# First attention's scores over all 128 rows, with key halves exchanged and queries doubled by on-chip transfers

## The reference, cut to what matters

```python
def project(t):                       # x: 256 tokens, context: 256 tokens
    p = t @ w_in                      # 1024 x 4096
    q, k, v, z = jnp.split(p, ...)    # q, k: 8 heads x 2 halves x 64; v: 8 heads x 128; z: 1024
q, k = apply_rope(q), apply_rope(k)   # x's tokens alone
k_all = concat([k, kc]); v_all = concat([v, vc])       # 512 keys

def diff(qq, kk, vv, gate):
    o1 = sweep_attention(qq[..., 0, :], kk[..., 0, :], vv)   # softmax(q k^T / 8) v
    o2 = sweep_attention(qq[..., 1, :], kk[..., 1, :], vv)
    o = rms_norm(o1 - lam * o2, subln_g) * (1 - lam_init)
    ...                               # times silu(z), then w_out
y = diff(q, k_all, v_all, z)          # x attends over x and context: 512 keys
yc = diff(qc, kc, vc, zc)             # context attends over context: 256 keys
```

## Time and profile before

| | |
|---|---|
| median of 3 runs | 780.48 us (780.07 to 780.59) |
| the profiled execution | 780.35 us, its span 778.3 us |
| TensorE busy (share of the span) | 765.4 us (98%), 4137 matmuls |
| TensorE weight loads | 613.8 us (79%) |
| VectorE | 550.9 us (71%) |
| ScalarE | 392.4 us (50%) |
| chain that ended last, by engine | TensorE 73%, VectorE 16%, ScalarE 3%, transfers 3% |
| of it, score matmuls of the first attention (L1067) | 3% |

### The profile page before, as it was taken

The page is one execution under the profiler, slowest core; times in us unless marked ns, Lnnn a source line. Parts: engine busy times, 40 slices in busy tenths (PEclk is TensorE's granted clock), DMA queues, the critical chain, the costliest instruction groups (busy, mean ns, idle before and its releaser), DMA issues.

```text
span 778.3 us, 11220 instructions
## 1 busy us (share of the span) xinstructions
PE 765.4 (98%) x4137; PEld 613.8 (79%) x4137; DVE 550.9 (71%) x985; ACT 392.4 (50%) x749; POOL 42.5 (5%) x55
## 2 busy tenths in 40 slices
PE   8999999999999999999999999999999999999998
PEld 6668777887777788867788888787788888888886
DVE  3456998987677867599757766998977554555553
ACT  4452222328788765566656656625444444444441
POOL 0120000000001010112100002200100000000000
PEclk9999999999999999999999999999999999999999
DMA  9995554333000085249222055963325855665621
GB/s 325 361 379 191 207 216 167 116 121 137 2 1 1 1 314 209 71 152 340 76 92 74 6 175 166 365 221 107 100 69 183 270 163 164 204 209 182 203 67 55
DMA packets 72409, 125.78 MB, mean 162 GB/s; under 512 B 2842, under 2 KB 36844, under 8 KB 71204
## 3 DMA queue, kind: packets, MB, share of 16 engines
q1 hardware_dynamic: 71504, 123.00, 45.9%
q10 hardware_dynamic: 388, 1.08, 0.4%
q0 software_dynamic: 464, 0.98, 0.4%
HBM read 123.99 MB, written 1.06 MB: 161 GB/s over the span
## 4 chain that ended last, share of the span: by engine, by line
PE 73%; DVE 16%; ACT 3%; DMA 3%; issue 2%; SPq 1%; POOL 1%; DVEq 0%; ACTq 0%
PE psum L871 15%; PE psum L873 14%; PE psum L872 14%; DVE w_lo L2004 5%; PE psum L1067 3%; PE psum L1092 3%; PE psum L1388 3%; PE psum L1387 3%; PE psum L1386 3%; PE psum L993 2%; PE psum L860 2%; PE psum L1165 2%; PE psum L861 2%; PE psum L862 2%; DMA kT<-in_ada_w 2%
## 5 line engine op out<-in xcount | busy, mean ns | idle before, releaser
L872 PE MATMUL psum<-w_lo,act_hi 128*128 128x512 f32 (+1 forms) x624 | 242.1, 388 | 0.0
L871 PE MATMUL psum<-w_hi,act_hi 128*128 128x512 f32 (+1 forms) x584 | 237.4, 407 | 2.9 <-DVE act_lo L2187 2.5
L873 PE MATMUL psum<-w_hi,act_lo 128*128 128x512 f32 (+1 forms) x584 | 226.9, 388 | 0.0
L2004 DVE TENSOR_TENSOR w_lo<-raw,w_hi 128x2048 fp32r<-128x2048 f32 (+1 forms) x68 | 153.2, 2261 | 62.3 <-ACT w_hi L1425 62.3
L1425 ACT ACTIVATE w_hi<-raw 128x2048 fp32r<-128x2048 f32 (+1 forms) x72 | 136.2, 1894 | 67.5 <-PE psum L873 30.9
L871 PEld LDWEIGHTS psum<-w_hi,act_hi 128*128 128x128 f32 x584 | 109.7, 188 | 37.7 <-issue 13.5
L872 PEld LDWEIGHTS psum<-w_lo,act_hi 128*128 128x128 f32 x624 | 117.5, 188 | 20.4 <-issue 0.5
L873 PEld LDWEIGHTS psum<-w_hi,act_lo 128*128 128x128 f32 x584 | 109.6, 188 | 23.3
L1973 POOL TENSOR_TENSOR rstd<-ms,half_neg 128x1 f32<-128x1 f32 (+3 forms) x38 | 36.0, 950 | 521.5 <-DVE ms L2045 521.5
L860 PE MATMUL psum<-act_hi,w_hi 128*128 128x512 f32 x128 | 50.7, 396 | 1.7 <-DVE w_lo L2004 1.7
L861 PE MATMUL psum<-act_lo,w_hi 128*128 128x512 f32 x128 | 50.0, 390 | 0.0
(11 more groups left out here) (295 smaller groups left out, 1123.0 us busy)
## 6 DMA issues: line engine op xcount, KB each, us to landing
raw<-in_a_w_in SPq DMA_DIRECT2D x16, 1024.0 KB, 8.7
raw<-in_ada_w SPq DMA_DIRECT2D x14, 1024.0 KB, 5.1
raw<-in_w_out SPq DMA_DIRECT2D x12, 1024.0 KB, 5.4
raw<-in_w_gate SPq DMA_DIRECT2D x22, 512.0 KB, 4.2
raw<-in_w_up SPq DMA_DIRECT2D x22, 512.0 KB, 5.3
raw<-in_w_down SPq DMA_DIRECT2D x11, 1024.0 KB, 4.9
raw<-in_b_w_in SPq DMA_DIRECT2D x10, 1024.0 KB, 7.5
raw<-in_w_in SPq DMA_DIRECT2D x10, 1024.0 KB, 6.0
```

The costliest lines, as they stand in the source:

```text
L871: pe.matmul(oh, x_hi, hi, start=(k == 0), stop=False)
L872: pe.matmul(o[:, 0:n], x_hi, lo, start=False, stop=False)
L873: mm = pe.matmul(oh, x_lo, hi, start=False, stop=(k == KT - 1))
L2004: ins = dve.tensor_tensor(rest, weights, hi.bitcast(F32), ALU.subtract)
```

## The change

Four pairs of heads have halves of their keys exchanged in place: what was the rounded part of the second half (rows 64 to 127 of `round_k`) and the rest of the first half (rows 0 to 63 of `rest_k`) change places, by way of `taken`. Then `round_k` of a head holds rounded and rest of its first half, one above the other on 128 rows, and `rest_k` those of its second half. The queries are laid out to match: for each pair of steps eight transfers write, for each half s, the rounded queries of that half on both the lower and the upper 64 rows, and the rests likewise, into one slot of `w_lo` that is kept for this by an entry `("doubled", 0, 0)` of the plan of loads. A step's scores are then, for each half, two matmuls on 128 rows: doubled rounded queries by (rounded, rest) keys, doubled rests by the same keys. This adds the product of rest by rest, which was left out before. All transfers are issued by SP, in its order between the weight loads; SP waits between the phases of an exchange. TensorE waits for the exchange of the heads and for the doubled queries before each step's scores.

```diff
@@ loads_plan
         if c == 4:
             plan += both("ada0g", 1)
+        elif c == 6:
+            plan.append(("doubled", 0, 0))
@@
+EXCHANGED_BEFORE = {("in0", 6, 0): [0, 1], ("doubled", 0, 0): [2], ("in0", 7, 0): [3]}
+
+
+DOUBLED_BEFORE = {("in0", 7, 1): [2], ("out0", 0, 0): [3], ("out0", 0, 1): range(4, 9), ("out0", 1, 0): range(9, 16)}
@@ emptied
-            if stage == "ada0g":
+            if stage == "doubled":
+                b, at = place[("s0", NT * HEADS - 1, 1)]
+                emptied[n] = (full[b], at + 1)
+            elif stage == "ada0g":
                 emptied[n] = (s_sumused, h + 1)
@@
+        LOW, HIGH = slice(0, 64), slice(64, P)
+        doubled_at = load_no[("doubled", 0, 0)] % RAW
+        doubled = w_lo[:, doubled_at, :].rearrange("p (s r i n) -> p s r i n", s=2, r=4, i=2)
@@ SP
+            def exchange(pair):
+                heads = slice(2 * pair, 2 * pair + 2)
+                last = HEADS + 2 * pair + 1
+                b, at = place[("in0", BY_FEATURES[0] + last // NT, last % NT)]
+                sp.wait_ge(s_rest0, last + 1)
+                sp.wait_ge(free[b], at + 1)
+                aside = taken[:].rearrange("p t n -> p (t n)").bitcast(F32)
+                for i, half in enumerate((LOW, HIGH)):
+                    sp.dma_start(aside[half], round_k[HIGH, 2 * pair + i, :].bitcast(F32)).then_inc(s_exchanged, 16)
+                sp.wait_ge(s_exchanged, 96 * pair + 32)
+                for h in (2 * pair, 2 * pair + 1):
+                    sp.dma_start(round_k[HIGH, h, :].bitcast(F32), rest_k[LOW, h, :].bitcast(F32)).then_inc(s_exchanged, 16)
+                sp.wait_ge(s_exchanged, 96 * pair + 64)
+                for i, half in enumerate((LOW, HIGH)):
+                    sp.dma_start(rest_k[LOW, 2 * pair + i, :].bitcast(F32), aside[half]).then_inc(s_exchanged, 16)
+                if pair < HALF_KT - 1:
+                    sp.wait_ge(s_exchanged, 96 * pair + 96)
+
+            def doubled_queries(pair):
+                t, h = STEPS0[2 * pair]
+                if pair == 0:
+                    sp.wait_ge(s_rest0, HEADS)
+                elif pair >= 2:
+                    b, at = place[("s0", 2 * pair - 3, 1)]
+                    sp.wait_ge(full[b], at + 1)
+                r = slice(2 * (pair % 2), 2 * (pair % 2) + 2)
+                tokens = round_q[:, h, :].rearrange("p (s t n) -> p s t n", s=2, t=XT)[:, :, t, :].bitcast(F32)
+                rests = rest_q[:, 2 * pair:2 * pair + 2, :].bitcast(F32)
+                for s, own in enumerate((LOW, HIGH)):
+                    for half in (LOW, HIGH):
+                        sp.dma_start(doubled[half, s, r, 0, :].bitcast(F32), tokens[own]).then_inc(s_doubled[pair % 2], 16)
+                        sp.dma_start(doubled[half, s, r, 1, :].bitcast(F32), rests[own]).then_inc(s_doubled[pair % 2], 16)
@@ SP, over the loads
+                for pair in EXCHANGED_BEFORE.get(loads[n], ()):
+                    exchange(pair)
+                if loads[n][0] == "doubled":
+                    sp.wait_ge(*emptied[n - RAW])
+                    for pair in range(2):
+                        doubled_queries(pair)
+                    continue
+                for pair in DOUBLED_BEFORE.get(loads[n], ()):
+                    doubled_queries(pair)
@@ TensorE, scores0
-                o = [begin(("s0", p, s)) for s in range(2)]
-                for i in range(3):
-                    for s in range(2):
-                        rows = slice(64 * s, 64 * s + 64)
-                        q = rest_q[rows, p, :] if i == 2 else round_q[rows, h, tile_cols(t)]
-                        k = (rest_k if i == 1 else round_k)[rows, h, keys]
-                        mm = pe.matmul(o[s][:, 0:n], q, k, start=(i == 0), stop=(i == 2))
-                        if i == 2:
-                            mm.then_inc(bank_full(("s0", p, s)), 1)
+                pe.wait_ge(s_doubled[p // 2 % 2], 128 * (p // 4 + 1))
+                pe.wait_ge(s_exchanged, 96 * (h // 2 + 1))
+                for s in range(2):
+                    o = begin(("s0", p, s))
+                    k = (round_k, rest_k)[s][:, h, keys]
+                    for i in range(2):
+                        mm = pe.matmul(o[:, 0:n], doubled[:, s, p % 4, i, :], k, start=(i == 0), stop=(i == 1))
+                    mm.then_inc(bank_full(("s0", p, s)), 1)
```

More of the change, by code:

```diff
@@ L302, in block_kernel @@
     load_no = {key: n for n, key in enumerate(loads)}
-    halves = [key for key in loads if not key[0].startswith("ada")]
+    halves = [key for key in loads if not key[0].startswith("ada") and key[0] != "doubled"]
     half_no = {key: g for g, key in enumerate(halves)}
@@ L450, in block_kernel @@
         s_gatein = sem("first_gate_chunk_in")
+        s_exchanged = sem("key_halves_exchanged")
+        s_doubled = [sem(f"doubled_queries{i}") for i in range(2)]
         N_CIN, N_VEC, N_LATE = 3, 4, 10
@@ L582, in block_kernel @@
         for n, (stage, c, h) in enumerate(loads):
-            n_landed[n % RAW] += 32 if stage == "gu" else 16
+            n_landed[n % RAW] += 32 if stage == "gu" else 0 if stage == "doubled" else 16
             landed_at[n] = n_landed[n % RAW]
```

## The result

The changed kernel takes 793.24 us (793.14 to 793.37, four runs) against 780.54 us for the kernel before (780.07 to 780.93, four runs): 1.0161 times, interval 1.0149 to 1.0174. It is 12.7 us slower, and 17.4 us above the forecast of 775.8. The profiled execution took 793.26 us with a span of 791.3.

A forecast was written before the change was run, and what follows sets the result against it. TensorE's matmul stream was taken to bound the changed stretch. From 780.35 us, less 6.5 for the scores, plus 1.7 idle before the first score and 0.3 for other engines: 775.85, so 775.8; range 773.4 to 781.5.

The forecast's parts named there:

- the chain on SP: SP's queue of exchanges, weight loads and doubled queries: pair 0's queries land at 171.1, TensorE wants them at 169.38, idles 1.7 us.
- The price of the products: TensorE in the loop: heavy step 2.24 to 2.07 us, light step 1.20 to 0.94; 15 pairs gain 6.5 us.
- the rival of the costly fourth slot: Scores: the fourth slot costs and the change of rows doesn't; each pair loses 0.35 us, 787.3 us in all; chance 0.04.
- Does another engine take over in the loop?: Chain from light scores to heavy transposes: four pairs beside a rounded weight half lose most of their gain, 0.3 us in all.
- The rival that a second engine binds: VectorE or ScalarE becomes the loop's bound, shares 82% and 85%; 778.8 us if every pair waited 0.2 us; chance 0.07.
- The forecast's own sign for it: TensorE idle before the transposes, released by VectorE, over 0.3 us in all, would mean the other engines took over.
- the landing: Time for an on-chip transfer to land: taken as 2.1 us, nearest to the final stores, bounds 2.0 and 2.9.
- About 1 us of cover; no cost: Pair 2's doubled queries land at about 184, its scores want them at 185.1, so TensorE doesn't wait there.
- The clock: Rival: the idle at 169.4 lowers TensorE's clock to 1.2 GHz for 10 us, some 5 us: 780.9 or 782; chance 0.03.
- The rival of the slow exchange: Eight landings in series before the first score at 2.9 us each, 6.4 us more: 782.2 us; chance 0.20, 0.07 of it slower.
- The lower end of the range: 773.4 us for the whole kernel, said to be the hidden exchange with the low bounds.

## Why the prediction was wrong

It forecast 775.8 us and had 781.5 as its upper end; 793.24 came. What failed above all is the chain on SP: it gave the first score a wait of 1.7 us and the scores of pair 2 none, and the runs showed 7.5 and 4.1, with a restart at the lower clock behind each. By its own steps:

- *The price of the products held.* 2.06 and 0.93 for forecast 2.07 and 0.94; the rival of the costly fourth slot is out. The starts of the earlier trace rows were the right place to read it from. This fits what the Trainium skill, TensorEngine Tiling (Array Packing), Key Properties, says of a drain when the tiling mode changes; no run here shows the drain apart from the other effects of the 64-row products.
- *"Does another engine take over in the loop?" failed, worth 4.2 us.* The forecast was 6.5 - 0.3 = 6.2; the run without transfers gives 2.0 over the loop (100.55 - 98.57: its first transposes come 0.10 later and those of step 30 1.88 earlier than before). The step followed one chain, up to the heavy transposes, and priced its cover at the earlier trace rows. It never followed the other, transposes to ScalarE's copy to the values, although TensorE takes that copy in every step. The rival that a second engine binds had 778.8 and a chance of 0.07; it is what happened, by waits for a place in ScalarE's order and not by its share of busy time. The forecast's own sign for it was sought before the transposes; the waits stood before the values.
- *The SP chain had the right links and sizes that were too small, worth 5.8 us at the first score.* Third exchange done at 170.4 for forecast 166.2, queries landed at 177.5 for 171.1. Of these 6.4 us the largest term is the issue of the queries: eight need seven pitches of 0.71 at the mean, (175.45 - 170.49) / 7, instead of 0.40, 2.2 us. Seven phases took 2.83 (144.20 - 141.37) instead of 2.55, 2.0 us. The first exchange's first phase was 1.0 us later, and chunk 6 with the third exchange's first phase took 9.3 us (155.51 to 164.85) instead of 8.0. (The forecast's 160.2 for the landing of chunk 6 was already 0.6 above its own terms, 154.2 + 5.4, so the miss there is larger than it looks.) A phase was 0.50 for the second issue and up to 2.3 to land, for 0.40 and 2.1. The forecast said that the landing would decide, with 2.0 to 2.9 as bounds; on-chip transfers with nothing ahead of them landed in 2.0 to 2.3, inside. What had no bound is the pitch of the issues, read where the queue was short, and the landing behind weight loads.
- *"About 1 us of cover; no cost" for pair 2 failed, worth 4.1 us.* From pair 0's last issue to pair 2's it forecast 12.4 us (169.0 to 181.4), and it was 194.37 - 175.45 = 18.9: two more groups of eight at the larger pitch and an exchange between them. A cover of 1 us behind a chain of 23 issues whose pitch was not known should have carried a range.
- *The clock, given 0.03, came true, worth 3.1 us.* 1.53 and 1.60 us behind the two waits. It was treated as a rival with its own small chance, but it hangs on how long the wait is: the idles of 7.4 and 3.9 us brought it, those of 3.1 us and of 1.0 did not. The rival had taken 10 us at the lower clock and 5 us of loss; the rows have 3.5 us and 1.6 for each wait.
- *Remainder.* 5.8 + 4.1 + 3.1 + 4.2 and the 0.6 by which the changed kernel is late already at the first score make 17.8, less 0.3 won back behind; 17.4 were to be explained. The 0.6 are there before the first on-chip transfer, and the same place lies up to 2 us apart from trace to trace, so they aren't put down to the change.
- *The rival of the slow exchange* named the right place and had 782.2, but by another mechanism: landings of 2.9 us in series. Its 6.4 us of lateness are the measured 6.4 by luck; the landings were 2.0 to 2.3, and pitch and weight loads made the rest. On two transfers to disjoint halves of the partitions the Trainium skill, DMA: Bandwidth & Descriptors, Rules for kernel authors, says that they serialize. This case can't tell: the two of a phase are issued 0.50 us apart, longer than the 0.33 us that 128 KB take at the 394 GB/s of the earlier trace rows, and landed 2.2 and 2.3 us after their issue.
- *The lower end of the range*, 773.4, doesn't come out of the low bounds that it names; they give about 774.0. This has no part in the miss.

The range was too narrow for one reason: the bounds were put on the landing, the number that looked unknown, and the pitch, the wait behind weight loads and the copies' cover got none.

## What to carry to other kernels

Moving work from an engine to transfers puts it on the issuing queue: count its issues at the pitch of issues that follow each other there, and its waits, and ask whether an idle engine can issue them. Here the same transfers cost 14.6 us on SP and 1.1 with a part of them on GpSimd. Before a gain on the bounding engine is booked, follow every operand that it takes in the loop back to its producer and read its cover; here VectorE and ScalarE were busy for about 80% of the loop at most, and still only 2.0 of the 6.2 us forecast for it came while the values had to wait for a copy. A step that only feeds a later sum can stand last in its engine's order, but one on which others wait can't.

## What the runs showed of the hardware

- A weight load holds SP 0.37 us where it stands alone and 0.59 among query transfers; an on-chip transfer mostly 0.46 to 0.51 alone or first after a wait and 0.60 to 0.65 behind others, for 32, 64 or 128 rows. GpSimd held 0.52 us for each of its own.
- A transfer within the on-chip memory of 64 KB or 128 KB landed in 1.8 to 2.3 us where little else moved, in 2.0 to 5.6 us (medians about 3) for the query transfers of the changed kernel up to 200 us, the longest with others and weight loads under way, and in 7.7 to 7.8 behind two 1 MB loads on SP's queue. Issued by GpSimd while SP's loads moved it took up to 6.2.
- After an idle of 7.4 and of 3.9 us TensorE worked mostly at the lower clock through the next 3.5 us, which cost 1.5 and 1.6 us. After an idle of 3.1 us, in the run with 64-row scores and all transfers, it worked at the full one.
- A transfer share of 0.49 instead of 0.08 over the loop did not slow TensorE's products: pairs of 2.95 + 3.21 us are found in the changed kernel (211.59 to 217.75) as in the one without transfers (209.36 to 215.52).
